# Stick-breaking value blocks first, token tile by token tile, with the norm's weight row spread by TensorE

## Chip, cores and metric

One core of a Trainium2 chip runs the kernel. The metric is the device time of one execution in microseconds (us); the times given are medians of runs. Engines: TensorE (PE) multiplies, VectorE (DVE), ScalarE (ACT) and GpSimd (POOL) compute element by element, SyncE (SP) issues most DMAs.

## Reference

A decoder block on 256 tokens of width 1024, and a second block behind it. Only the head of the first one matters here:

```
def rmsnorm(x, g):
    xf = x.astype(jnp.float32)
    y = xf * lax.rsqrt(jnp.mean(xf * xf, axis=-1, keepdims=True) + EPS)
    return (y * g.astype(jnp.float32)).astype(x.dtype)
...
        h = rmsnorm(x, norm_mix[l])
        (fq, fk, fv, ff, gq, gk, gv, gb, ga, gz, sq, sk, sv, gates) = split_projection(h @ w_in[l])
        ...
        ya = fox_attention(fq, fk, heads(fv, FOX_HEADS), logf)
        ...
        o = gated_delta_rule(l2norm(heads(cq, GDN_HEADS)), l2norm(heads(ck, GDN_HEADS)),
                             heads(cv, GDN_HEADS), g_log, beta)
        ...
        yc = stick_breaking_attention(heads(sq, SB_HEADS), heads(sk, SB_HEADS), heads(sv, SB_HEADS))
```

In the stick-breaking branch the scores z are q times k; log_keep is minus the softplus of z; its sums over the later keys are added to z, and the exp of that multiplies the values sv. In the delta rule a triangular 64 x 64 system per chunk is solved. Everything is float32.

## Kernel before

The weights stream through the core once, in 187 blocks of 1 MB, in the order of the table PHASES (name, number of blocks). Block n goes through three buffers: a DMA on SyncE's queue puts each half (512 KB) into RAW (two slots), ScalarE rounds it to HI (four slots), VectorE makes LO = RAW - HI. A product is then three matmuls: HI with x's high part XH, LO with XH, HI with XL. A slot of RAW is free for block n + 2 once LO of block n is there. HI and LO of block n + 4 are made by the calls `split_ahead` on ScalarE and VectorE, placed by hand behind the work on block n. Each engine runs its program strictly in the order in which it is written, and semaphores join them.

Blocks come in forms: f (`f_gemm`: 48 matmuls of 256 tokens, output by channel, used for gdn, sbqk and the gates) and t (`t_part` for one token tile, `t_half` for both: 24 matmuls of 512 columns, output by token, used for sbv, foxqk, foxv). Products of blocks go to the four PSUM banks ACCP; `_accumulations` says which. Small things go to the four banks SMP, in turn, in the order of the list SMALL: a name waits until the name four places before it has been taken out of its bank.

The opening: SyncE loads x in two tiles of 128 tokens, then the norm's weight row norm_mix spread over all partitions (PRE_GAIN, 512 KB written), then gdn's first two blocks, then small rows. ScalarE sums the squares, POOL forms the root, VectorE scales (`norm_scale`, two halves a tile), TensorE transposes (`norm_turn`), ScalarE copies to XH and VectorE subtracts to XL (`norm_split`, per quarter). Ahead of that TensorE runs seven warm-up products (WARM_UP).

The middle, on TensorE: six gdn blocks, four sbqk blocks with the delta rule's transposes between them, sbv block 0, the small products kk and kq (four names of SMP), sbv block 1, the scores z0 to z3, foxqk 0 to 2, `rest_sums` for two heads (waits for keep_ready), foxqk 3, the other two heads, foxv 0 and 1, the products so (exp of the sticks times SV), gate_c 0, T16, gate_c 1, the transposes fT of the fox heads.

Beside it VectorE takes kk into delta_L (DL) and kq into delta_AT (MAT), forms SP_ from z (keep_abs, then keep_ready after ScalarE's exp and ln), and solves the 16 x 16 diagonal blocks (diag_L, diag_T, 30 small instructions), whose data SyncE moves through DRAM: eight writes of delta_L, a read into diag_L, and after the solve a write and eight reads into delta_P. The weight loads behind them in SyncE's queue wait for it.

Of the kernel before, what the change touches and what calls it, by code (L numbers as in the profile page):

```python
# [52 lines left out]
    ("gdn", 6), ("sbqk", 4), ("sbv", 2), ("foxqk", 4), ("foxv", 2),  # L53
# [34 lines left out]
def _accumulations():  # L88
# [9 lines left out]
    for phase, count in PHASES:  # L98
# [84 lines left out]
def build(nc, A, out):  # L183
# [24 lines left out]
    with ctx:  # L208
# [73 lines left out]
        TINY = at("TINY", 26, [P, SEQ])  # L282
        TW = at("TW", 80, [P, KT, 12])
# [82 lines left out]
        sumsq, scaled, norm_hi = sems("sumsq scaled norm_hi")  # L366
        tiny_hi, tiny_lo, tiny_abs, tiny_ln, tiny_sp, tiny_exp = sems("tiny_hi tiny_lo tiny_abs tiny_ln tiny_sp tiny_exp")
# [156 lines left out]
        def _(sp):  # L524
# [54 lines left out]
            for j in range(RAWS, 6):  # L579
                load("gdn", Turn(j), f_block(w["w_in"], C_GQKV + 256 * j))  # L580
            load_f("sbqk", w["w_in"], C_SQ)
            load_t("sbv", w["w_in"], C_SV)
# [62 lines left out]
        def _(pool):  # L645
# [18 lines left out]

            pool.memset(BROW, 0.0).then_inc(bias_zeroed, 1)
# [130 lines left out]
        def _(pe):  # L796
# [26 lines left out]
            def t_part(phase, j, m, xh, xl, ready=None):  # L823

                chunk, half = Turn(j // 2), j % 2
                s = lo_is_ready(pe, phase, Turn(j))
                if half == 0:
                    acc_banks_free(pe, phase, chunk, m)
                for k in range(4):
                    kk = 4 * half + k  # L830
                    if ready:
                        ready(kk)
# [135 lines left out]

            for _ in range(WARM_UP):
                pe.matmul(SMP[:, 3, 0:P], IDENT[:, :], IDENT[:, :], start=True, stop=True)  # L970
            for t in range(NT):
                norm_turn("norm_mix", XS, t)

            for j in range(6):
                f_gemm("gdn", Turn(j), XH, XL, norm_ready("norm_mix", 0, 1) if j == 0 else None)
# [43 lines left out]
            t_half("sbv", 0, XH, XL)  # L1019
# [6 lines left out]
            t_half("sbv", 1, XH, XL)  # L1026

# [7 lines left out]
            for j in range(3):  # L1035
                t_half("foxqk", j, XH, XL)
# [32 lines left out]
            f_gemm("gate_c", Turn(0), XH, XL)  # L1069
# [318 lines left out]
        def _(act):  # L1388
# [71 lines left out]
            for t in range(NT):  # L1460
                act.wait_ge(x_loaded[t], 16)
                norm_square("norm_mix", t, X, XS)
            for t in range(NT):
                norm_split("norm_mix", t, XH)
                split(0, (t,))
            for n in range(1, RING):
                split(n)
            act.wait_ge(tiny_w_loaded, 16 * 2)
            copy(THI[:, :, :], TW[:, :, :], tiny_hi)


# [99 lines left out]
            split_ahead("gate_c", Turn(0))  # L1571
            take_small("T16_0", ME[:, 0], by_head(small("T16_0")))
# [337 lines left out]
        def _(dve):  # L1910
# [42 lines left out]
            def norm_scale(r, t, src, dst):  # L1953

                dve.wait_ge(pre_gain_loaded, 16 * (NORMS.index(r) + 1))
                root = root_is_ready(f"{r}.{t}")
                for half in (slice(0, DM // 2), slice(DM // 2, DM)):
                    dve.scalar_tensor_tensor(out=dst[:, t, half], in0=src[:, t, half], scalar=root,
                                             in1=PRE_GAIN[:, half], op0=ALU.mult, op1=ALU.mult).then_inc(scaled, 1)

            def norm_split(r, t, hi, lo):

                for b in range(2):
# [26 lines left out]
            for t in range(NT):  # L1990
                dve.wait_ge(x_loaded[t], 16)
                norm_scale("norm_mix", t, X, XS)
            for t in range(NT):
                norm_split("norm_mix", t, XH, XL)
                split(0, (t,))
            split(1)

# [9 lines left out]
            for n in range(2, RING):  # L2007
                split(n)
            dve.wait_ge(tiny_hi, 1)
            dve.tensor_tensor(TLO[:, :, :], TW[:, :, :], THI[:, :, :].bitcast(f32), ALU.subtract).then_inc(tiny_lo, 1)  # L2010

# [57 lines left out]
            split_ahead("sbv", Turn(0))  # L2069
# [10 lines left out]
            split_ahead("sbv", Turn(1))  # L2080
# [3 lines left out]

            dve.wait_ge(diag_loaded, 16)
# [11 lines left out]
            split_ahead("foxqk", Turn(0))  # L2097
# [4 lines left out]
            split_ahead("foxqk", Turn(1))  # L2102

            split_ahead("foxqk", Turn(2))

# [454 lines left out]
```

## Time and profile before

| what | us |
|---|---|
| median of 3 timed runs | 1183.82 (1183.72 to 1186.32) |
| the profiled execution | 1186.28 |
| its span, first to last instruction | 1184.3 |
| TensorE busy | 1158.5 (98%) |
| VectorE busy | 738.5 (62%) |
| ScalarE busy | 595.0 (50%) |

All times in rows are of the profiled execution, from the start of its span. Busy time of TensorE counts overlapping pipelined matmuls, so 98% does not mean that it is at its peak.

### The profile page before, as it was taken

To read this page: it belongs to the slowest core of one execution; us is meant where nothing else is said; L and a number is where in the kernel's file an instruction comes from. 1 tells how busy PE (TensorE), PEld (TensorE's weight loads), DVE (VectorE), ACT (ScalarE), POOL (GpSimd) and SP (SyncE) were. 2 spreads that over 40 slices of the span, in tenths; PEclk is the share of its full clock that TensorE was granted. 3 is DMA by queue.
4 is the path that set the end of the run, shared out by engine and by line. 5 is a ranking of instruction groups with operands and counts; after the bars stand their busy time and mean duration, and the time that the engine had idled before them with its cause. 6 is when DMAs were issued, how large, how long until landed. Compare 5 with 4: busy or idle time off the path is not lost.

```text
span 1184.3 us, 19550 instructions
## 1 busy us (share of the span) xinstructions
PE 1158.5 (98%) x7788; PEld 1070.6 (90%) x7788; DVE 738.5 (62%) x912; ACT 595.0 (50%) x799; POOL 96.1 (8%) x156
## 2 busy tenths in 40 slices
PE   7999999999999999999999999999999999999997
PEld 7998799999888999988999998799888899999885
DVE  5767656557766788764665544565775566554455
ACT  5675544345555665652544443464473365443352
POOL 5310211001010000000000000200400010000011
PEclk9999999999999999999999999999999999999999
DMA  8744453446553675565565646565475458655641
GB/s 238 214 128 128 145 178 107 137 148 198 197 191 114 222 218 177 177 213 178 167 209 178 194 161 211 156 217 165 123 245 179 160 149 273 191 178 178 199 139 70
DMA packets 150287, 208.77 MB, mean 176 GB/s; under 512 B 10944, under 2 KB 113485, under 8 KB 150221
## 3 DMA queue, kind: packets, MB, share of 16 engines
q1 hardware_dynamic: 147053, 199.18, 53.9%
q10 hardware_dynamic: 3072, 8.65, 2.1%
q8 instruction: 48, 0.79, 0.3%
q0 software_dynamic: 96, 0.01, 0.1%
q14 instruction: 18, 0.15, 0.0%
HBM read 206.63 MB, written 1.18 MB: 175 GB/s over the span
## 4 chain that ended last, share of the span: by engine, by line
PE 88%; DVE 6%; ACT 3%; DMA 2%; issue 1%; POOL 1%; SPq 0%; POOLq 0%; DVEq 0%; ACTq 0%
PE ACCP L799 25%; PE ACCP L801 25%; PE ACCP L800 25%; DVE LO L1922 3%; PE SMP L950 2%; PE SMP L943 2%; PE SMP L799 2%; PE SMP L800 2%; PE SMP L801 2%; ACT HI L1411 1%; DMA PRE_GAIN<-in_norm_mix_dram 1%; DMA diag_L<-scratch_diag_l 1%; DMA RAW<-in_w_out_b_dram 0%; PE ACCP L920 0%; DVE U L2444 0%
## 5 line engine op out<-in xcount | busy, mean ns | idle before, releaser
L1922 DVE TENSOR_TENSOR LO<-RAW,HI 128x1024 fp32r<-128x1024 f32 x367 | 438.3, 1233 | 238.6 <-ACT HI L1411 236.9
L1411 ACT ACTIVATE HI<-RAW 128x1024 fp32r<-128x1024 f32 x366 | 369.1, 1054 | 233.2 <-PE ACCP L801 201.5
L799 PE MATMUL ACCP<-XH,HI 128*128 128x256 f32 x1408 | 401.2, 285 | 1.9 <-DVE XL L1967 1.9
L801 PE MATMUL ACCP<-XH,LO 128*128 128x256 f32 x1408 | 399.1, 283 | 0.0
L800 PE MATMUL ACCP<-XL,HI 128*128 128x256 f32 x1408 | 399.0, 283 | 0.0
L799 PEld LDWEIGHTS ACCP<-XH,HI 128*128 128x128 f32 x1408 | 270.8, 192 | 2.4 <-DVE LO L1922 2.2
L800 PEld LDWEIGHTS ACCP<-XL,HI 128*128 128x128 f32 x1408 | 270.9, 192 | 0.0
L801 PEld LDWEIGHTS ACCP<-XH,LO 128*128 128x128 f32 x1408 | 270.8, 192 | 0.0
L799 PE MATMUL ACCP<-HI,HH 128*128 128x512 f32 x328 | 128.8, 393 | 1.9 <-DVE HL L2463 1.9
L801 PE MATMUL ACCP<-HI,HL 128*128 128x512 f32 x328 | 128.4, 392 | 0.0
L800 PE MATMUL ACCP<-LO,HH 128*128 128x512 f32 x328 | 128.3, 391 | 0.0
L799 PE MATMUL ACCP<-HI,XH 128*128 128x512 f32 x272 | 107.0, 393 | 2.3 <-ACT SV L1419 1.6
L801 PE MATMUL ACCP<-HI,XL 128*128 128x512 f32 x272 | 105.9, 390 | 0.0
L800 PE MATMUL ACCP<-LO,XH 128*128 128x512 f32 x272 | 105.9, 389 | 0.0
L676 POOL TENSOR_SCALAR STAT<-STAT 128x1 f32<-128x1 f32 (+3 forms) x30 | 10.0, 334 | 807.7 <-ACT XS L1665 461.8
L799 PEld LDWEIGHTS ACCP<-HI,HH 128*128 128x128 f32 x328 | 62.0, 189 | 14.8 <-issue 2.0
L801 PEld LDWEIGHTS ACCP<-HI,HL 128*128 128x128 f32 x328 | 61.9, 189 | 13.0
L800 PEld LDWEIGHTS ACCP<-LO,HH 128*128 128x128 f32 x328 | 62.0, 189 | 12.7
L799 PEld LDWEIGHTS ACCP<-HI,XH 128*128 128x128 f32 x272 | 51.1, 188 | 13.2 <-issue 1.7
L801 PEld LDWEIGHTS ACCP<-HI,XL 128*128 128x128 f32 x272 | 51.0, 188 | 10.8
L800 PEld LDWEIGHTS ACCP<-LO,XH 128*128 128x128 f32 x272 | 51.1, 188 | 10.1
L799 PE MATMUL SMP<-HI,XH 128*128 128x256 f32 x160 | 45.6, 285 | 1.5 <-DVE XL L1967 1.1
(375 smaller groups left out, 1320.4 us busy)
## 6 DMA issues: line engine op xcount, KB each, us to landing
RAW<-in_w_in_dram SPq DMA_DIRECT2D x104, 512.0 KB, 4.6
RAW<-in_w_up_dram SPq DMA_DIRECT2D x44, 512.0 KB, 4.5
RAW<-in_ffn_w_gate_dram SPq DMA_DIRECT2D x44, 512.0 KB, 4.5
RAW<-in_ffn_w_up_dram SPq DMA_DIRECT2D x44, 512.0 KB, 4.6
RAW<-in_ffn_w_down_dram SPq DMA_DIRECT2D x44, 512.0 KB, 4.2
RAW<-in_w_down_dram SPq DMA_DIRECT2D x22, 512.0 KB, 4.2
RAW<-in_w_out_dram SPq DMA_DIRECT2D x8, 512.0 KB, 4.2
RAW<-in_w_mkv_dram SPq DMA_DIRECT2D x8, 512.0 KB, 4.2
```

Of the source, the lines that this page charges most:

```text
L676: link(pool.tensor_scalar(mean_square, mean_square, EPS, None, ALU.add))
L799: pe.matmul(dst, lhs[0], rhs[0], start=start, stop=False)
L800: pe.matmul(dst, lhs[0], rhs[1], start=False, stop=False)
L801: return pe.matmul(dst, lhs[1], rhs[0], start=False, stop=stop)
L943: last = pe.matmul(small(name)[:, h * P:(h + 1) * P], lhs, rhs, start=True, stop=True)
L950: last = pe.transpose(small(name)[:, h * P:(h + 1) * P], source(h), IDENT[:, :])
L1411: act.activation(HI[:, n % RING, half_of(half)], RAW[:, n % RAWS, half, :], ACT.Copy).then_inc(hi_ready, 1)
L1922: dve.tensor_tensor(LO[:, s, c], RAW[:, n % RAWS, half, :], HI[:, s, c].bitcast(f32), ALU.subtract).then_inc(lo_ready[s], 1)
```

## The change

The two sbv blocks become the first of all blocks and are multiplied tile by tile: as soon as x's first tile is normed, both sbv blocks are run on it, then both on the second tile. gdn follows, on both tiles; its PSUM banks are shifted by two. SyncE's load order is x tile 0, sbv 0, x tile 1, sbv 1, the small rows, gdn. The weight row is no longer loaded spread: ScalarE's queue loads it as one row of 4 KB (GAIN_ROW), and TensorE multiplies a row of ones with it, once per 512 columns, into the idle banks 2 and 3 of ACCP, from which `norm_scale` reads it. In the middle, foxqk 0 takes the place of sbv 0, nothing stands between kq and z, and foxqk, foxv and gate_c 0 move one place ahead.

```diff
 PHASES = [
-    ("gdn", 6), ("sbqk", 4), ("sbv", 2), ("foxqk", 4), ("foxv", 2),
+    ("sbv", 2), ("gdn", 6), ("sbqk", 4), ("foxqk", 4), ("foxv", 2),
...
-                acc(phase, j, j, (j + (phase in PAIRS) * 2) % 4)
+                acc(phase, j, j, (j + (phase in PAIRS or phase == "gdn") * 2) % 4)
```

SyncE's loads:

```diff
             for t in range(NT):
                 sp.dma_start(X[:, t, :], A["x"][0, tok(t), :]).then_inc(x_loaded[t], 16)
-            sp.dma_start(PRE_GAIN[:, :], A["norm_mix"].broadcast_to([P, DM])).then_inc(pre_gain_loaded, 16)
-            for j in range(RAWS):
-                load("gdn", Turn(j), f_block(w["w_in"], C_GQKV + 256 * j))
+                load("sbv", Turn(t), t_block(w["w_in"], C_SV, t))
```

GpSimd:

```diff
+            pool.memset(ONE_ROW[:, :], 1.0).then_inc(one_row_ready, 1)
```

TensorE:

```diff
+            for b in range(2):
+                pe.matmul(ACCP[:, 2 + b, :], ONE_ROW[:, :], GAIN_ROW[:, b * 512:(b + 1) * 512], start=True, stop=True).then_inc(gain_spread, 1)
             for _ in range(WARM_UP):
                 pe.matmul(SMP[:, 3, 0:P], IDENT[:, :], IDENT[:, :], start=True, stop=True)
-            for t in range(NT):
-                norm_turn("norm_mix", XS, t)
+            for m in range(NT):
+                norm_turn("norm_mix", XS, m)
+                for j in range(2):
+                    last = t_part("sbv", j, m, XH, XL, norm_ready("norm_mix", m), by_half=m == 0)
+                    if m == 1:
+                        last.then_inc(block_done, 1)
...
-            t_half("sbv", 0, XH, XL)
+            t_half("foxqk", 0, XH, XL)
...
-            t_half("sbv", 1, XH, XL)
-
...
-            for j in range(3):
+            for j in range(1, 4):
                 t_half("foxqk", j, XH, XL)
...
-            t_half("foxqk", 3, XH, XL)
+            t_half("foxv", 0, XH, XL)
             for h in range(2, 4):
                 rest_sums(h)
-            for j in range(2):
-                t_half("foxv", j, XH, XL)
+            t_half("foxv", 1, XH, XL)
+            f_gemm("gate_c", Turn(0), XH, XL)
...
-            f_gemm("gate_c", Turn(0), XH, XL)
```

ScalarE:

```diff
+            act.dma_start(GAIN_ROW[:, :], A["norm_mix"]).then_inc(gain_row_loaded, 16)
+            act.wait_ge(x_loaded[0], 16)
+            norm_square("norm_mix", 0, X, XS)
+            split(0)
+            norm_split("norm_mix", 0, XH)
+            act.wait_ge(x_loaded[1], 16)
+            norm_square("norm_mix", 1, X, XS)
+            split(1)
+            norm_split("norm_mix", 1, XH)
...
-            split_ahead("sbv", Turn(0))
-
-            for half in range(2):
-                split_ahead("sbv", Turn(1), (half,))
-                for h in ((0,), (1, 2, 3))[half]:
-                    take_small(f"z{h}", Z[:, h, :], small(f"z{h}")[:, 0:384])
-            take_t("sbv", 0, SV)
             split_ahead("foxqk", Turn(0))
+            for h in range(HEADS):
+                take_small(f"z{h}", Z[:, h, :], small(f"z{h}")[:, 0:384])
...
+            take_t("foxv", 0, FV)
+            split_ahead("foxv", Turn(1))
             for h in range(HEADS):
                 small_is_taken(act, f"rc{h}")
             act.activation(Z[:, :, :], Z[:, :, :], ACT.Exp).then_inc(stick_ready, 1)
-            take_t("foxv", 0, FV)
-            split_ahead("foxv", Turn(1))
```

VectorE:

```diff
+            dve.wait_ge(x_loaded[0], 16)
+            norm_scale("norm_mix", 0, X, XS)
+            for half in range(2):
+                split(0, (half,))
+                norm_split("norm_mix", 0, XH, XL, (half,))
             split(1)
+            dve.wait_ge(x_loaded[1], 16)
+            norm_scale("norm_mix", 1, X, XS)
+            norm_split("norm_mix", 1, XH, XL)
...
-            split_ahead("sbv", Turn(0))
+            split_ahead("foxqk", Turn(0))
...
-            split_ahead("sbv", Turn(1))
             for h in range(HEADS):
                 small_is_taken(dve, f"z{h}")
             dve.scalar_tensor_tensor(out=SP_[:, :, :], in0=Z[:, :, :], scalar=-1.0, in1=Z[:, :, :], op0=ALU.mult, op1=ALU.max).then_inc(keep_abs, 1)
 
+            split_ahead("foxqk", Turn(1))
             dve.wait_ge(diag_loaded, 16)
...
             ins.then_inc(diag_solved, 1)
-            split_ahead("foxqk", Turn(0))
             dve.wait_ge(keep_ln, 1)
```

TensorE at the opening, before: four quarters of transposes, then gdn's first block (small_taken are the banks of SMP that XL's subtractions free, lo_ready0 is LO of block 0, scaled is VectorE's scaling).

```order
L950 MATMUL SMP<-IDENT,XS 128x128 [waits scaled]
L950 MATMUL SMP<-IDENT,XS 128x128 x3
L950 MATMUL SMP<-IDENT,XS 128x128 [waits scaled]
L950 MATMUL SMP<-IDENT,XS 128x128 x3
L799 MATMUL ACCP<-XH,HI 128x256 [waits small_taken2,small_taken0,lo_ready0]
L800 MATMUL ACCP<-XL,HI 128x256
L801 MATMUL ACCP<-XH,LO 128x256
```

The same place in the changed kernel, from its first matmul.

```order
L973 MATMUL ACCP<-GAIN_ROW,ONE_ROW 128x512 [waits gain_row_loaded,one_row_ready,masks_ready]
L973 MATMUL ACCP<-GAIN_ROW,ONE_ROW 128x512
L975 MATMUL SMP<-IDENT 128x128 x7
L951 MATMUL SMP<-IDENT,XS 128x128 [waits scaled]
L951 MATMUL SMP<-IDENT,XS 128x128 x3
L951 MATMUL SMP<-IDENT,XS 128x128 [waits scaled]
L951 MATMUL SMP<-IDENT,XS 128x128 x3
L798 MATMUL ACCP<-HI,XH 128x512 [waits small_taken0,lo_ready0]
L799 MATMUL ACCP<-LO,XH 128x512
L800 MATMUL ACCP<-HI,XL 128x512
```

The gain products stand ahead of the warm-ups, and the first weight product follows two quarters of transposes and waits for one quarter of x (small_taken0) instead of two.

TensorE around the scores z, before: the end of sbv block 1, z0 to z3 (L1032 and L1033), the start of foxqk 0.

```order
L801 MATMUL ACCP<-HI,XL 128x512
L1032 MATMUL SMP<-SQK 128x256 [waits acc_taken3,acc_taken2,small_taken2,acc_taken1,acc_taken0]
L1033 MATMUL SMP<-SQK 128x128
L1032 MATMUL SMP<-SQK 128x256 [waits small_taken3]
L1033 MATMUL SMP<-SQK 128x128
L1032 MATMUL SMP<-SQK 128x256 [waits small_taken0]
L1033 MATMUL SMP<-SQK 128x128
L1032 MATMUL SMP<-SQK 128x256 [waits small_taken1]
L1033 MATMUL SMP<-SQK 128x128
L799 MATMUL ACCP<-HI,XH 128x512 [waits acc_taken0,lo_ready0]
```

The same place in the changed kernel: the end of kq (L944), z (L1039 and L1040), the start of foxqk 1.

```order
L944 MATMUL SMP<-QKF 128x128 [waits small_taken1,small_taken3]
L944 MATMUL SMP<-QKF 128x128 x3
L1039 MATMUL SMP<-SQK 128x256 [waits acc_taken3,acc_taken2,small_taken2,acc_taken1,acc_taken0]
L1040 MATMUL SMP<-SQK 128x128
L1039 MATMUL SMP<-SQK 128x256 [waits small_taken3]
L1040 MATMUL SMP<-SQK 128x128
L1039 MATMUL SMP<-SQK 128x256 [waits small_taken0]
L1040 MATMUL SMP<-SQK 128x128
L1039 MATMUL SMP<-SQK 128x256 [waits small_taken1]
L1040 MATMUL SMP<-SQK 128x128
L798 MATMUL ACCP<-HI,XH 128x512 [waits lo_ready1]
```

What moved is the block between kq and z: none stands there now. The banks small_taken2, 3, 0 and 1 are those of kk0, kk1, kq0 and kq1.

VectorE behind kq, before: the kq products, LO of a block, the absolute value of z, the diagonal solve.

```order
L2079 TENSOR_TENSOR delta_AT<-SMP,delta_B 128x512 [waits small_done] x2
L1922 TENSOR_TENSOR LO<-RAW,HI 128x1024 [waits hi_ready] x2
L2083 SCALAR_TENSOR_TENSOR SP__72<-Z 128x1536 [waits small_taken0,small_taken1,small_taken3,small_taken2]
L2092 TENSOR_TENSOR diag_term<-diag_L,diag_T 64x15 [waits diag_zeroed,diag_loaded]
L2093 TENSOR_TENSOR diag_T<-diag_T,diag_term 64x15 [waits dve_step]
```

The same place in the changed kernel.

```order
L2097 TENSOR_TENSOR delta_AT<-SMP,delta_B 128x512 [waits small_done] x2
L2100 SCALAR_TENSOR_TENSOR SP__72<-Z 128x1536 [waits small_taken0,small_taken1,small_taken3,small_taken2]
L1932 TENSOR_TENSOR LO<-RAW,HI 128x1024 [waits hi_ready] x2
L2110 TENSOR_TENSOR diag_term<-diag_L,diag_T 64x15 [waits diag_zeroed,diag_loaded]
L2111 TENSOR_TENSOR diag_T<-diag_T,diag_term 64x15 [waits dve_step]
```

LO (now of the block four behind foxqk 1) stands behind the absolute value and ahead of the solve; the LO that stood between the solve and the keep sums is gone from there.

## Rows read from the trace of the kernel before

**Rows 1.** The page, part 1: busy time, share of the span, instructions.
```profile
PE 1158.5 (98%) x7788; PEld 1070.6 (90%) x7788; DVE 738.5 (62%) x912; ACT 595.0 (50%) x799; POOL 96.1 (8%) x156
```

**Rows 2.** TensorE's waits, whole span: us in total, times, longest.
```profile
PE SMP L1045 <- DVE SP__72 L2101: 2.2, 1, 2.2
```

**Rows 3.** Timeline, TensorE, opening: start, us, line, operation, count, idle before.
```profile
4.03 3.36 PE L970 MATMUL SMP<-IDENT 128*128 128x128 f32 x14 [4.03 <-POOL IDENT L655]
9.09 3.64 PE L950 MATMUL SMP<-IDENT,XS 128*128 128x128 f32 x16 [1.70 <-DVE XS L1958]
14.64 0.35 PE L799 MATMUL ACCP<-XH,HI 128*128 128x256 f32 x1 [1.91 <-DVE XL L1967]
```

**Rows 4.** Timeline of ScalarE, GpSimd and VectorE, opening.
```profile
4.45 1.06 ACT L1427 ACTIVATE XS<-X 128x1024 f32<-128x1024 f32 x1 [2.36 <-DMA X<-in_x_dram]
6.10 0.57 POOL L677 TENSOR_TENSOR STAT<-STAT 128x1 f32<-128x1 f32 x1
8.28 2.84 DVE L1958 SCALAR_TENSOR_TENSOR XS<-X,STAT,PRE_GAIN 128x512 f32<-128x512 f32 x4 [8.28 <-DMA PRE_GAIN<-in_norm_mix_dram]
11.04 1.38 DVE L1967 TENSOR_TENSOR XL<-SMP,XH 128x512 fp32r<-128x512 f32 x2
```

**Rows 5.** Windows of TensorE: length, busy (instructions), granted clock, DMA share, GB/s.
```profile
14.60:15.80 1.20, 1.16 (x10) 1.00 1.07 45
16.40:19.20 2.80, 2.80 (x14) 0.50 0.97 279
122.00:124.00 2.00, 2.00 (x7) 0.50 0.56 108
```

**Rows 6.** DMA issues from 95 to 125: count, KB each, median us to landing.
```profile
scratch_diag_l<-delta_L SPq DMA_DIRECT2D x8, 8.0 KB, 1.7
```

**Rows 7.** Timeline, TensorE, middle: kk and kq, z, first foxqk block, rest_sums.
```profile
89.86 3.73 PE L943 MATMUL SMP<-QKF 128*128 128x128 f32 x32
98.88 0.59 PE L1032 MATMUL SMP<-SQK 128*128 128x256 f32 x2
103.23 0.47 PE L799 MATMUL ACCP<-HI,XH 128*128 128x512 f32 x1 [1.57 <-ACT SV L1419]
121.97 0.69 PE L1045 MATMUL SMP<-BIG_NOT_BEFORE_R,IDENT_R 128*128 128x384 f32 x1 [2.17 <-DVE SP__72 L2101]
```

**Rows 8.** Timeline, ScalarE, middle.
```profile
90.05 2.18 ACT L1411 ACTIVATE HI<-RAW 128x1024 fp32r<-128x1024 f32 x2 [0.92 <-PE ACCP L801]
110.87 1.47 ACT L1547 ACTIVATE SP__72<-SP__72 128x1536 f32<-128x1536 f32 x1
115.05 1.06 ACT L1419 ACTIVATE X<-ACCP 128x512 f32<-128x512 f32 x2
116.00 2.01 ACT L1411 ACTIVATE HI<-RAW 128x1024 fp32r<-128x1024 f32 x2
```

**Rows 9.** Timeline, VectorE, middle.
```profile
94.44 2.15 DVE L2074 SCALAR_TENSOR_TENSOR delta_L<-SMP,STAT,delta_A 128x128 f32<-128x128 f32 x8
96.51 1.28 DVE L2079 TENSOR_TENSOR delta_AT<-SMP,delta_B 128x512 f32<-128x512 f32 x2
102.74 1.76 DVE L2083 SCALAR_TENSOR_TENSOR SP__72<-Z 128x1536 f32<-128x1536 f32 x1
109.18 0.17 DVE L2092 TENSOR_TENSOR diag_term<-diag_L,diag_T 64x15 f32<-64x15 f32 x1 [4.68 <-DMA diag_L<-scratch_diag_l]
116.45 2.35 DVE L1922 TENSOR_TENSOR LO<-RAW,HI 128x1024 fp32r<-128x1024 f32 x2
```

**Rows 10.** SyncE's queue in the timeline, then the chain of waits.
```profile
96.68 3.66 SPq L595 DMA_DIRECT2D scratch_diag_l<-delta_L  x8
103.18 5.98 DMA diag_L<-scratch_diag_l
```

**Rows 11.** Timeline, VectorE and ScalarE, behind foxv.
```profile
142.88 4.54 DVE L1982 TENSOR_TENSOR X<-X,STAT 128x1024 f32<-128x1024 f32 x2 [3.87 <-POOL STAT L677]
144.40 1.08 ACT L1419 ACTIVATE FV<-ACCP 128x512 f32<-128x512 f32 x2 [0.63 <-PE ACCP L801]
```

More of the change, by code:

```diff
@@ L282, in build @@
         TINY = at("TINY", 26, [P, SEQ])
+        GAIN_ROW, ONE_ROW = at("GAIN_ROW", 64, [1, DM]), at("ONE_ROW", 68, [1, P])
         TW = at("TW", 80, [P, KT, 12])
@@ L578, in _ @@
             sp.dma_start(TW[:, :, 4:12], tiny_rows[:, :, C_GB:C_GB + 8]).then_inc(tiny_w_loaded, 16)
-            for j in range(RAWS, 6):
-                load("gdn", Turn(j), f_block(w["w_in"], C_GQKV + 256 * j))
+            load_f("gdn", w["w_in"], C_GQKV)
             load_f("sbqk", w["w_in"], C_SQ)
-            load_t("sbv", w["w_in"], C_SV)
             load_t("foxqk", w["w_in"], C_FQ)
@@ L821, in f_gemm, with t_part @@
                 f_part(phase, t, xh, xl, slice(0, SEQ), ready).then_inc(block_done, 1)
-            def t_part(phase, j, m, xh, xl, ready=None):
+            def t_part(phase, j, m, xh, xl, ready=None, by_half=False):
                 chunk, half = Turn(j // 2), j % 2
-                s = lo_is_ready(pe, phase, Turn(j))
+                s = lo_is_ready(pe, phase, Turn(j), half=0 if by_half else 1)
                 if half == 0:
@@ L830, in t_part @@
                     kk = 4 * half + k
+                    if by_half and k == 2:
+                        lo_is_ready(pe, phase, Turn(j))
                     if ready:
@@ L1458, in softmax_exp @@
                 ins.then_inc(bank_of(name), 1)
[L1460 to L1466, printed above, removed]
+            act.dma_start(GAIN_ROW[:, :], A["norm_mix"]).then_inc(gain_row_loaded, 16)
[7 more added lines that the diff above has]
+            norm_split("norm_mix", 1, XH)
+            for n in range(2, RING):
                 split(n)
@@ L1469, in _ @@
             copy(THI[:, :, :], TW[:, :, :], tiny_hi)
+            split_ahead("sbv", Turn(0))
+            acc_is_done(act, "sbv", Turn(0))
+            for m in range(NT):
+                copy(SV[:, m], acc("sbv", Turn(0), m), acc_bank("sbv", Turn(0), m))
+            split_ahead("sbv", Turn(1))
             def conv_silu(j):
@@ L1562, in _ @@
             act.activation(Z[:, :, :], Z[:, :, :], ACT.Exp).then_inc(stick_ready, 1)
-            take_t("foxv", 0, FV)
-            split_ahead("foxv", Turn(1))
+            act.wait_ge(heads_ready, 4)
+            gates("gate_c", 0, G, 2)
+            split_ahead("gate_c", Turn(0))
             for g in range(2):
@@ L1953, in norm_scale, with norm_split @@
             def norm_scale(r, t, src, dst):
-                dve.wait_ge(pre_gain_loaded, 16 * (NORMS.index(r) + 1))
                 root = root_is_ready(f"{r}.{t}")
-                for half in (slice(0, DM // 2), slice(DM // 2, DM)):
+                for b, half in enumerate((slice(0, DM // 2), slice(DM // 2, DM))):
+                    if r == "norm_mix":
+                        dve.wait_ge(gain_spread, b + 1)
+                        gain = ACCP[:, 2 + b, :]
+                    else:
+                        dve.wait_ge(pre_gain_loaded, 16 * NORMS.index(r))
+                        gain = PRE_GAIN[:, half]
                     dve.scalar_tensor_tensor(out=dst[:, t, half], in0=src[:, t, half], scalar=root,
-                                             in1=PRE_GAIN[:, half], op0=ALU.mult, op1=ALU.mult).then_inc(scaled, 1)
-            def norm_split(r, t, hi, lo):
-                for b in range(2):
+                                             in1=gain, op0=ALU.mult, op1=ALU.mult).then_inc(scaled, 1)
+            def norm_split(r, t, hi, lo, quarters=range(2)):
+                for b in quarters:
                     name = f"{r}.{t}{b}"
@@ L2005, in _ @@
             link(dve.tensor_scalar(col("mq_norm"), col("mq_norm"), DH ** -0.5, None, ALU.mult))
[L2007 to L2010, printed above, removed]
+            split_ahead("sbv", Turn(1))
             for j in range(6):
@@ L2112, in _ @@
                 stick_arg(h)
-            split_ahead("foxqk", Turn(3))
+            split_ahead("foxv", Turn(0))
             for h in range(2, 4):
```

24 lines of the change are left out of this document (11 added, 13 removed).

## Prediction

> **What bounds the kernel now.** I read the page's engine shares first: TensorE is busy 98% of the span [rows 1], so a change pays only where TensorE stands or runs slowly, and costs wherever it makes TensorE stand. The view of TensorE's waits names the larger one in the middle: 2.2 us for the keep sums [rows 2], and the timeline 1.57 us for a PSUM bank that ScalarE had not yet emptied [rows 7]. It shows the rest too, at the opening: the warm-up products end at about 7.4, the transposes start at 9.09, and the first weight product only at 14.64 [rows 3]. The reader should see there that VectorE began scaling at 8.28, although the root of tile 0 was ready at 6.67: it had waited for the spread weight row [rows 4]. The windows give TensorE's clock: granted 1.00 (2.4 GHz) at 14.6, then 0.50 (1.2 GHz) from 16.4 to 19.2 after an opening with gaps, and 0.50 again at 122 to 124, after the 2.17 us wait [rows 5, 7]. In the slow stretch 14 products started in 2.8 us, against 10 in 1.2 us before it; the whole of it (about 15.9 to 19.2) cost some 1.6 us, and the one at 122 some 1.5.
>
> After 14.64 TensorE is nearly unbroken, so I count how late it is, phase by phase, against that timeline.
>
> **Term 1, the opening.** Removed: the 512 KB spread of the weight row. Added: a 4 KB load on ScalarE's queue, one POOL memset (0.1 us) and two K=1 products of 512 columns. No row shows such a load; the nearest are the 8 KB writes that landed in 1.7 us [rows 6] and the weight row itself, wanted by VectorE at 8.28 [rows 4]. So the row lands between about 3 and 8; I take 4, since it is small and early, and TensorE starts at 4.1 as now. A warm-up product is two passes of 128 columns; 14 passes took 3.36 us, 0.24 each [rows 3]. Four passes of 512 columns are then at most 3.8 us: the two halves of the gain are there at 6.0 and 7.9. The seven warm-ups behind them take 3.4 us if the clock stays low, half that if it rises; I take 10.0 for their end. VectorE scales half by half from 6.7 (0.75 each), the second half at 7.9. Transposes of the first quarter end at 10.9, ScalarE copies (0.6), VectorE subtracts (0.69, half of the row of 1.38) [rows 4]: 12.2, and the first block's first half starts, 2.4 us earlier than now.
>
> It doesn't run through. ScalarE turns to x's second tile only then (1.06 and 0.19, then two splits of 1.0 each), so the second block's low half is ready at 15.8; TensorE, done with the first at 15.0, waits 0.8, finishes at 18.5, transposes tile 1 (16 passes, 1.8), waits 0.5 for the subtraction, and ends both blocks of tile 1 at 26.3 (5.5 us of products). The two blocks are 11.0 us of work (three such blocks took 16.6, below), so this equals an unbroken start at 15.3. Now it is 14.64 plus 1.6 of slow clock, 16.2. Gain 0.9, plus 0.3 because the same two blocks now cost 5.7 each in the middle: **-1.2**. Bounds: -4.1 (start at 12.2 with no wait and no slow stretch behind), +2 (row lands near 8).
>
> **Term 2, the bank wait goes.** The first foxqk block waited 1.57 us for ScalarE's copies of SV [rows 7]; SV is now taken long before. **-1.6**.
>
> **Term 3, a new wait for z.** Let F be the moment when TensorE begins the kk products: 89.9 now, behind the first sbv block; in the change behind foxqk's first. kk and kq take 3.4. Now sbv's second block (5.7) stands behind them; in the change z follows at once. Each z takes the bank of one kk or kq, and VectorE empties those late: ScalarE's split begins at F+0.15 and takes 2.18, VectorE's low half follows, and its delta_L rows run at F+4.5 to F+6.6, its products on kq until F+7.9 [rows 8, 9]. So z0 starts at F+5.6, z1 at F+6.6, z3 at F+7.8. The four z end at F+8.5, where 3.4 + 2.6 (98.9 to 101.7 [rows 7]) would give F+6.0. **+2.5**. VectorE's program ahead of kk is unchanged in kind, so I see no cover for this one.
>
> **Term 4, the keep wait grows.** From the end of z, F+8.5: ScalarE copies the last z (0.5), VectorE forms the absolute value 1.76 [rows 9]: F+10.8. ScalarE's exp to the first foxqk copy is 4.2 (110.87 to 115.05), the copies 0.95, its split 2.0 [rows 8]: F+18.0. The order now puts that block's low half ahead of the diagonal solve: F+19.3. The diagonal data should be there: VectorE's delta_L ends at F+6.6, the eight writes issue in 3.7, the read took 6.0 behind a weight load [rows 10], so about F+18. The solve takes 7.3 (109.18 to 116.45), the keep sums 3.2 (118.8 to 121.97) [rows 7, 9]: F+29.8. TensorE has only three foxqk blocks to do, 103.23 to 119.80, that is 16.6 [rows 7]: it is free at F+25.1 and waits 4.8 us, not 2.2. **+2.6**. Bounds 0 (solve starts at F+16.7) and +4. Late next are the loads of gate_c's first two blocks, which SyncE issues behind the solve. By the same count they are split at about F+36 and F+41, wanted at F+48 and F+56: covered.
>
> **Term 5, gate_c block 0 behind foxv.** It takes a PSUM bank that foxv's first chunk just filled. ScalarE's two copies took 1.08 and began at once [rows 11]; the bank is free 0.6 later: **+0.6**. In return the exp of the sticks is hidden under gate_c; it was hidden before too.
>
> **Term 6, the transposes of HT.** VectorE waits 3.87 for POOL's root and scales for 4.54, ending at 147.4 [rows 11], 3 us behind the end of foxv. In the change it starts these some 7 to 10 us later relative to foxv, since its splits wait for late weights; ScalarE's gates, its next split and its copies of the stick outputs stand behind, and the banks the transposes want come free at about the moment they want them: 0 to 1.5, I take **+0.7**.
>
> **Term 7, the clock.** The keep wait is twice as long, and z's wait (2.2 us in one piece) resembles the one that was followed by the low level, while the 1.57 us wait was not. Slow products behind z are hidden by the keep wait; behind keep they are not: 0 to 2.5, I take **+0.9**.
>
> Phases from out_c on are the same program. Sum: -1.2 - 1.6 + 2.5 + 2.6 + 0.6 + 0.7 + 0.9 = **+4.5 us**. The profiled execution took 1186.28 with a span of 1184.3; the three timed runs have their median at 1183.82, so the sum goes on the median: 1188.3. A measurement of this kernel can tell about 0.3% (3.6 us) from no change.
>
> **Rivals.** *The opening runs clean.* The trace shows that TensorE could have had x 1.6 us earlier, and with the clock up from 12.2 term 1 is -4.1, term 7 nothing: +0.7, or 1184.5, not slower. Against it stand the waits of 0.8 and 0.5 worked out above. *The new waits don't come.* If VectorE empties kk and kq before z wants them and keep stays at 2.2, terms 3, 4 and 7 vanish: -1.5, or 1182.3; with a clean opening 1179.4, faster. The deciding point is F+3.4: VectorE would have to finish with kk0 by then, and in the rows it starts at F+4.5. *The low clock stays through the opening.* Transposes and warm-ups then take twice as long and the first 24 products too: q0's subtraction comes 2.2 later, and tile 0's products cost up to 2.7 more, part of it in waits: +3, or 1191.3. In the rows 16 transpose passes took 3.64 us (0.23 each), the low pace, yet the products at 14.6 ran at the high level [rows 3, 5]: the clock rose while nothing but warm-ups and transposes had run. The Trainium skill ("TensorE: Matmul & The Clock Gate", Part 4: PE-mode transpose) says that transposes don't count as activity for raising the clock. By that rule the clock would still be low at the first products, as in this rival; the trace of before doesn't agree, since the level was 1.00 at 14.6, but the change puts two real products ahead, so neither reading makes it much likelier.
>
> **Chances.** Forecast 0.55 (its own range 1185 to 1192), clean opening 0.18, no new waits 0.15, low clock 0.12. Above 1187.4 lie the low clock and most of the forecast (0.45): 0.57. Below 1180.3 lies half of the case without waits and a sliver of the clean opening: 0.11. The rest is 0.32. The range of 8 in 10 runs from 1180.5 to 1193: it takes in most of the case without waits, and at the top the low clock with the upper bound of term 4.
>
> **What would show it.** Right: first ACCP product of XH near 12.2; gdn's first block near 26.3; a wait of about 2.2 before the z products on VectorE's delta_L; a wait near 4.8 before the keep sums; 0.6 before gate_c's first block. Wrong: no wait at z (then VectorE's program is ahead of where I place it), or a solve that starts before the foxqk split. The forecast fails most easily if the opening gains more than 3 us.

## The result

The changed kernel takes 1193.01 us (median of 4 runs, 1190.49 to 1194.48); the kernel before takes 1183.77 in the same measurement (4 runs, 1182.28 to 1186.32). The ratio is 1.0083, 95% interval 1.0067 to 1.0098: 9.2 us slower, where the forecast was 4.5. The profiled execution took 1190.49, with a span of 1188.8; it is the fastest of the four, and the profiled one of before (1186.28) is one of the slowest of its kernel. So the two traces differ by only 4.5 us. A second trace of each differs by 8.9, the size of the measured loss; most of the reading below uses those two. They are called *before, second trace* (label b_again) and *after, second trace* (a_again).

**Busy time** is what it was [rows 1]. The page of the changed kernel:

```profile
PE 1159.6 (98%) x7792; PEld 1069.4 (90%) x7792; DVE 739.0 (62%) x912; ACT 595.4 (50%) x799; POOL 97.7 (8%) x157
```

TensorE is busy 1.1 us longer in a span that is 4.5 us longer; busy time counts slow products too, so the clock is in it, and the rest is standing. **TensorE's waits** behind its start, in the first 200 us (us in total, times, longest), answer to [rows 2]:

```profile
PE SMP L1052 <- DVE SP__72 L2118: 5.1, 1, 5.1
PE SMP L1039 <- DVE delta_L L2092: 2.1, 1, 2.1
PE ACCP L798 <- DVE XL L1982: 1.7, 2, 1.1
PE ACCP L798 <- ACT FV L1425: 0.8, 1, 0.8
```

L1052 is rest_sums waiting for the keep sums, L1039 z waiting for the kk bank, and the last row gate_c's first block. All three are where the prediction put them, with 4.8, 2.2 and 0.6. The wait for SV of [rows 7] is not in the list. **The opening**, TensorE's timeline, beside [rows 3]:

```profile
4.06 3.77 PE L973 MATMUL ACCP<-GAIN_ROW,ONE_ROW 1*128 1x512 f32 x4 [4.06 <-POOL IDENT L653]
7.76 3.35 PE L975 MATMUL SMP<-IDENT 128*128 128x128 f32 x14
10.91 1.91 PE L951 MATMUL SMP<-IDENT,XS 128*128 128x128 f32 x8
13.48 0.47 PE L798 MATMUL ACCP<-HI,XH 128*128 128x512 f32 x1 [0.65 <-DVE XL L1982]
```

The row had landed before TensorE wanted it. The seven warm-ups ran at the low pace to the end, so the transposes begin at 10.91 and not at 10.0. The first weight product is at 13.48, not 12.2, and the products behind it run at full pace, 0.23 from start to start (kk_first below has another opening). **The middle**, beside [rows 7]:

```profile
100.82 3.73 PE L944 MATMUL SMP<-QKF 128*128 128x128 f32 x32
106.66 0.67 PE L1039 MATMUL SMP<-SQK 128*128 128x256 f32 x2 [2.11 <-DVE delta_L L2092]
109.59 0.48 PE L798 MATMUL ACCP<-HI,XH 128*128 128x512 f32 x1
131.28 0.69 PE L1052 MATMUL SMP<-BIG_NOT_BEFORE_R,IDENT_R 128*128 128x384 f32 x1 [5.10 <-DVE SP__72 L2118]
```

With F = 100.82 the z products begin at F+5.8 (predicted F+5.6) and rest_sums at F+30.5 (predicted F+29.8). VectorE shows the order behind both waits, beside [rows 9]: the split of the weights, then delta_L; later another split, then the first step of the solve.

```profile
103.12 2.36 DVE L1932 TENSOR_TENSOR LO<-RAW,HI 128x1024 fp32r<-128x1024 f32 x2
105.40 2.15 DVE L2092 SCALAR_TENSOR_TENSOR delta_L<-SMP,STAT,delta_A 128x128 f32<-128x128 f32 x8
118.53 2.36 DVE L1932 TENSOR_TENSOR LO<-RAW,HI 128x1024 fp32r<-128x1024 f32 x2 [6.27 <-ACT HI L1417]
120.81 0.16 DVE L2110 TENSOR_TENSOR diag_term<-diag_L,diag_T 64x15 f32<-64x15 f32 x1
```

**The clock** is where the traces of one kernel part ways. Windows (length, busy and instructions, granted clock, DMA share, GB/s) of the first trace of before,

```profile
16.00:18.50 2.50, 2.50 (x13) 0.50 0.95 258
122.00:125.00 3.00, 3.00 (x10) 0.50 0.53 91
886.50:889.50 3.00, 3.00 (x8) 0.50 0.46 171
```

of its second trace,

```profile
16.00:18.50 2.50, 2.50 (x14) 0.50 0.92 259
122.00:124.00 2.00, 1.67 (x10) 1.00 0.80 197
886.00:889.00 3.00, 3.00 (x15) 1.00 0.39 127
```

of the first trace of the changed kernel,

```profile
106.50:109.50 3.00, 2.79 (x15) 1.00 0.05 8
131.50:133.50 2.00, 2.00 (x8) 0.50 1.11 353
```

and of its second trace.

```profile
16.00:18.50 2.50, 2.40 (x11) 1.00 1.05 342
108.00:111.00 3.00, 3.00 (x12) 0.50 0.13 14
132.00:136.00 4.00, 3.37 (x11) 0.50 0.89 256
```

In both traces of before the level falls to 0.50 (1.2 GHz) in the opening. The stretches at 122 and 886, some 1.5 us each, stood in the first one only. The changed kernel has none in the opening in either trace, one of 7 us behind the keep wait in both, and in the second trace one on the z products too. The second trace of before has the same two waits in the middle (keep 2.56, SV 1.57) without a low level behind them.

### The profile page after: what moved, and what is told of

It is laid out like the page before. It is cut to its first block, busy times and chain, and to the rows that moved or that the text cites. A ratio compares the mean times of both kernels' runs of the same rounds, so it can differ in the third digit from the quotient of the medians.

```text
span 1188.8 us, 19557 instructions
## 1 busy us (share of the span) xinstructions
PE 1159.6 (98%) x7792; PEld 1069.4 (90%) x7792; DVE 739.0 (62%) x912; ACT 595.4 (50%) x799; POOL 97.7 (8%) x157
## 4 chain that ended last, share of the span: by engine, by line
PE 85%; DVE 7%; ACT 4%; issue 1%; POOL 1%; DMA 1%; POOLq 0%; DVEq 0%; ACTq 0%
PE ACCP L798 25%; PE ACCP L800 24%; PE ACCP L799 24%; DVE LO L1932 3%; PE SMP L951 2%; ACT HI L1417 2%; PE SMP L798 2%; PE SMP L800 2%; PE SMP L799 2%; PE SMP L944 1%; POOL STAT L676 1%; DMA RAW<-in_w_in_dram 1%; DMA RAW<-in_w_out_b_dram 0%; PE ACCP L921 0%; DVE XS L1973 0%
## 5 line engine op out<-in xcount | busy, mean ns | idle before, releaser
L798 PEld LDWEIGHTS ACCP<-HI,HH 128*128 128x128 f32 x328 | 61.6, 188 | 14.6 <-issue 2.2
```

The costliest lines, as they stand in the source:

```text
L798: pe.matmul(dst, lhs[0], rhs[0], start=start, stop=False)
```

## Experiments

Each is compared with the kernel before on its own chip; ratios are to before, so that kernels timed on different chips can be set side by side.

**The two kernels again.** No edit.

> The changed kernel, unaltered, timed again on one chip beside the kernel before, for its spread and a second trace. Known: +4.2 us between the two profiled executions (1190.49 against 1186.28), +9.2 between the medians. Theory A (clock): the waits before z (2.1) and before the keep sums (5.1) are the same in each execution, but the clock falls after them, or in the opening, in some executions and not in others; then this trace shows the same waits within 0.3 us and more slow clock than the first one, and the median is +8 to +10. Rival B (noise between the two sets of runs): the median comes to +4 to +6. Rival C (the opening): its first gdn block starts 2 us or more later than at 27.2.

> The kernel before, unaltered, for a second trace. Its first profiled execution (1186.28) was 2.5 above its median. Theory A: the second trace has the same two waits (1.6 and 2.2) and less slow clock, in the opening or behind the keep wait (each stretch cost about 1.5). Rival B: same clock stretches, and a span within 1 us of 1184.3. The ratio of its times to those of the kernel before must be 1.000 within 0.1%.

The changed kernel: 1191.68, ratio 1.0075 (1.0058 to 1.0092). Before against itself: 1182.21, ratio 0.9999 (0.9988 to 1.0011). Over the whole execution the mean granted clock was 0.994 or 0.995 in all six of the changed kernel, and 0.992 to 0.998, with its median at 0.996, in the 17 of before beside them: 0.2% of 1184 is 2.4 us. The loss repeats, as theory A had it, and part of it is in the clock. The mean clock also says how usual the first trace of before is: it had 0.994, and 14 of those 17 had 0.996 or more.

**keep_first**: the keep sums ahead of the split and the solve on VectorE.

```
             keep_abs ...
+            dve.wait_ge(keep_ln, 1)
+            ... the three keep sums ... .then_inc(keep_ready, 1)
             split_ahead("foxqk", Turn(1))
             dve.wait_ge(diag_loaded, 16)
             ... the solve ...
-            ... the keep sums ...
```

> The changed kernel with VectorE's three keep-sum instructions moved ahead of the foxqk split and the diagonal solve. The keep sums can then start when ScalarE's ln is ready (about F+15) and end by F+18.5, before TensorE is free at F+25. Theory A: the wait of 5.1 and the slow clock behind it (2.4) go, -7 to -8 us against the changed kernel, so +1 to +2.5 against the kernel before. Rival D (the wait only moves: the solve and its weight loads, now 3 us later, stall gate_c): -3 to -5 only, with a new wait of 2 us or more behind foxv.

1191.89, ratio 1.0081 (1.0062 to 1.0100): nothing gained. Rival D, that the wait only moves, was right in kind, but expected 3 to 5 us to be left. TensorE's waits behind 90 us:

```profile
PE ACCP L798 <- ACT FV L1425: 5.5, 1, 5.5
PE SMP L951 <- DVE YL L2003: 1.2, 1, 1.2
```

The keep wait is gone, z waits 2.1 as in the changed kernel, and gate_c's first block waits 5.5 instead of 0.8. SyncE's queue and ScalarE say why:

```profile
113.08 0.53 SPq L595 DMA_DIRECT2D diag_L<-scratch_diag_l  x1
129.34 0.46 SPq L597 DMA_DIRECT2D scratch_diag_t<-diag_T  x1
129.84 1.17 SPq L535 DMA_DIRECT2D RAW<-in_w_in_dram  x2
134.77 1.06 ACT L1417 ACTIVATE HI<-RAW 128x1024 fp32r<-128x1024 f32 x1 [15.33 <-DMA RAW<-in_w_in_dram]
146.09 1.06 ACT L1425 ACTIVATE FV<-ACCP 128x512 f32<-128x512 f32 x2
```

SyncE stands from 113.6 to 129.3 for the solve, and the weights of gate_c's block 0 are queued behind it. ScalarE waits 15.3 us for them, and its copy of FV, which frees the bank, stands behind that split. The real chain is: solve, SyncE's loads, ScalarE's order, PSUM bank. It was there in the changed kernel too, hidden behind the keep wait: ScalarE stood 4.4 us for TensorE ahead of the same copy (149.06). Here TensorE is done with foxv 7.7 us earlier (141.3 against 149.0), while ScalarE is free for the copy only at 146.1, where it was free at 144.6 there.

**kk_first**: the kk and kq work of VectorE ahead of its split of block 16, four behind foxqk 0 (`split_ahead("foxqk", Turn(0))` moved behind the kq loop).

> The changed kernel with VectorE's kk and kq work moved ahead of the split of the block four behind foxqk 0. VectorE then empties kk's banks by F+4.2 instead of F+6.6. The wait before z (2.1) should go. The chain from the end of z to the keep sums is 21.3 us long and shifts with it, and TensorE's work between them does too, so the keep wait stays at about 5. Theory A: -2.3 us, and less than that by nothing hidden. Rival E (the keep wait is bound by the diagonal data, not by z): the keep wait grows by the 2.3 that z gives, and the time stays.

1188.36, ratio 1.0045 (1.0028 to 1.0061), 3.3 us below the changed kernel on the same chip. z follows kq at once (105.56), with the clock up; the keep wait is 5.52. The two waits together are 1.6 shorter (5.5 against 2.1 and 5.0), so some 1.7 us came back otherwise; I put it on the clock on z, as the difference, not as a reading.

This trace holds something else. Its edit touches nothing in the opening, but the first products are slow there:

```profile
13.48 0.77 PE L798 MATMUL ACCP<-HI,XH 128*128 128x512 f32 x1 [0.65 <-DVE XL L1982]
14.04 0.63 PE L799 MATMUL ACCP<-LO,XH 128*128 128x512 f32 x1
14.47 0.63 PE L800 MATMUL ACCP<-HI,XL 128*128 128x512 f32 x1
```

The step is 0.43 until 17.0, and gdn and everything behind it come 1.2 us later than in the first trace of the changed kernel (kk at 101.98 against 100.82). The seven other traces with this opening ran at full pace from 13.48 or so, with gdn's first block at 27.0 to 27.3. So the changed kernel too has a low pace in its opening in some executions.

**warm**: the changed kernel with products that nobody reads, in its two pauses.

```
+            for _ in range(9): pe.matmul(ACCP[:, 2, 0:P], IDENT, IDENT)     (ahead of z)
             for h in range(HEADS):
...
+            acc_is_taken(pe, "foxqk", Turn(0))
+            for _ in range(21): pe.matmul(ACCP[:, 0, 0:P], IDENT, IDENT)    (ahead of the keep wait)
             pe.wait_ge(keep_ready, 1)
```

> The changed kernel with products that nobody reads put into its two new pauses: 9 of 128 columns ahead of the z products and 21 ahead of the keep sums, so that TensorE has something to do while it waits. No wait is shortened. If the low clock behind the waits is a cost of its own (stretches of 3.4 us at half pace, in two traces of three on the z products and behind the keep sums in all three, each worth 1.5 to 3.4 us of products), it vanishes and the time falls by 2 to 4 us against the changed kernel on the same chip, to about 1188.5, with no stretch at 0.50 between 100 and 145 us. If only the length of the waits counts, the time stays within 0.7 us of it.

1188.14, ratio 1.0042 (1.0029 to 1.0055), against 1.0075 without the fillers: 3.9 us by the ratios (1.4 to 6.4 by their intervals together). Between the profiled spans it is 4.3 against the second trace (1186.3 and 1190.6) and 2.5 against the first (1188.8), which had no low level on z. TensorE's timeline and windows:

```profile
104.29 2.17 PE L1038 MATMUL ACCP<-IDENT 128*128 128x128 f32 x18
125.92 4.85 PE L1049 MATMUL ACCP<-IDENT 128*128 128x128 f32 x42
131.22 0.45 PE L1057 MATMUL SMP<-BIG_NOT_BEFORE_R,IDENT_R 128*128 128x384 f32 x1 [0.44 <-DVE SP__72 L2123]
```

```profile
108.00:111.00 3.00, 3.00 (x19) 1.00 0.16 17
131.50:135.00 3.50, 3.50 (x21) 1.00 0.79 224
```

z starts at 106.49 and rest_sums at 131.22, no earlier than in the first trace without fillers (106.66 and 131.28). The waiting is all there, but filled, and the level doesn't fall behind it. So about 4 us is the price of the low clock behind the two waits, beside the waits themselves.

**keep_early**: keep_first, and SyncE issues gate_c's loads 0 and 1 before it waits for the solve. **both_early**: that with kk_first. **both_early2**: that with gate_c's load 2 ahead of the eight reads of the solved diagonal.

```
             sp.dma_start(DIAG_L ...).then_inc(diag_loaded, 16)
+            for j in range(2): load("gate_c", Turn(j), ...)                 (and no longer behind the solve)
             sp.wait_ge(diag_solved, 1)
             sp.dma_start(diag_t ..., DIAG_T ...).then_inc(diag_stored, 16)
+            load("gate_c", Turn(2), ...)                                    (both_early2 alone)
```

> The changed kernel with the keep sums ahead of the block split and the solve (as in keep_first), and with SyncE issuing the loads of gate_c's blocks 0 and 1 before it waits for the solve instead of behind it. If the late loads behind the solve are what ate the gain of keep_first, the wait of gate_c's first block (5.5 us there) falls to 1 us or less, the keep wait stays away, and the time falls by 5 to 7 us against the changed kernel: 1185 to 1187. If the gain goes on to a next wait (the T16 transposes behind a later solve, or the transposes of HT), it falls by at most 2 us and that wait shows 3 us or more.

> As keep_early, and with the kk and kq work of VectorE ahead of the low half of block 16 (as in kk_first), so that z has no wait either. If both waits, with their low clock, are the whole loss of the change and the removed SV-bank wait a real gain, this ends 8 to 11 us below the changed kernel: 1181 to 1183.5, not slower than the kernel before and up to 1 us faster. If the opening of the change costs something too, it stays 2 us or more above the kernel before.

> As both_early, and with gate_c's third load ahead of the eight reads of the solved diagonal on SyncE's queue. There a wait of 2.1 us for ScalarE's copy of FV was left, behind a split that waited 9.2 us for that load, with a stretch at 0.50 after it. If that is the last of the chain, the wait falls to 0.8 or less and the time by 2 to 3.6 us against both_early, to 1181.6 to 1183.2, level with the kernel before or up to 1 us faster. If the eight reads, now later, hold up the T16 transposes, the time stays at 1185.

keep_early: 1188.33, ratio 1.0044 (1.0032 to 1.0056). both_early: 1185.21, ratio 1.0016 (1.0004 to 1.0029). both_early2: 1179.82, ratio 0.9975 (0.9963 to 0.9986). keep_early gained less than I expected, 3.7 us, for gate_c still waited 2.1 and z kept its wait. both_early came to 7.0 us below the changed kernel by the ratios, where I expected 8 to 11. both_early2 went further down than expected, 1179.82 against 1181.6 to 1183.2. In both_early ScalarE shows the next load in the chain, two places ahead of its copy of FV; both_early2 stands behind it:

```profile
137.75 1.06 ACT L1420 ACTIVATE HI<-RAW 128x1024 fp32r<-128x1024 f32 x1 [9.19 <-DMA RAW<-in_w_in_dram]
```

```profile
132.60 1.06 ACT L1421 ACTIVATE HI<-RAW 128x1024 fp32r<-128x1024 f32 x1 [3.96 <-DMA RAW<-in_w_in_dram]
138.87 1.09 ACT L1429 ACTIVATE FV<-ACCP 128x512 f32<-128x512 f32 x2 [3.37 <-PE ACCP L804]
```

In the second it is ScalarE that waits for TensorE at FV, and gate_c's wait is back at the 0.8 that the shared bank costs. In its window from 140 to 144 the granted clock is 1.00, where both_early had 0.50 from 142. The step gave 4.9 us by the ratios' difference for a wait 1.3 us shorter. By the two traces the clock gave more back than the wait did: both_early's had a low stretch behind the wait and another at 886, and this one's had neither. The T16 transposes come at 148.06, 3.3 us before the 151.39 of before's second trace. both_early2 is 0.25% below the kernel before. It doesn't say what the value blocks at the head are worth by themselves, since the kernel before was not given orders and loads fitted in the same way.

**gain_only**: the kernel before, its weight row spread by TensorE (4 KB on ScalarE's queue and the two K=1 products, in place of the 512 KB load).

> The kernel before with one part of the change alone: the first norm's weight row comes as 4 KB and is spread by two TensorE products into idle PSUM banks, in place of the 512 KB load. By my term for the opening the scaling starts 1.6 us earlier and the second half waits for the second product (7.9): the first weight product comes 1 to 1.5 us earlier than 14.6 and the time falls by about 1 us (ratio 0.999). If the weights' own arrival sets the start, the first product stays within 0.4 us of 14.6 and the time is the same.

1183.67, ratio 1.0006 (0.9996 to 1.0016): no change that can be told, and the expected gain of 1 us is not there. TensorE's timeline:

```profile
10.90 3.20 PE L952 MATMUL SMP<-IDENT,XS 128*128 128x128 f32 x16
16.41 0.36 PE L801 MATMUL ACCP<-XH,HI 128*128 128x256 f32 x1 [2.30 <-DVE XL L1979]
```

Against [rows 3] the transposes are 1.8 later and so is the first product, since the two spread products (3.8 us) push the warm-ups back. VectorE scales at 7.04 instead of 8.28, which is worth nothing, for TensorE isn't free until 10.9. A kernel with the spread products in place of the warm-ups was not run.

**row_not_spread**: the changed kernel with the 512 KB load again, first on ScalarE's queue.

> The changed kernel without its spread by TensorE: the weight row comes as the 512 KB load again, but first on ScalarE's queue instead of behind x on SyncE's; the value blocks stay first. In gain_only the two spread products pushed the warm-ups and transposes back, and the phases behind came 1.7 us later. If that is so here too, the transposes come before 10.9 and the first weight product at 12.5 or less instead of 13.48, and the time falls by 1 to 1.5 us against the changed kernel. If the weights' halves and ScalarE's order set the opening of the change, its first gdn block starts within 0.4 us of 27.1 as now and the time is the same.

1191.55, ratio 1.0063 (1.0050 to 1.0076), not told apart from the changed kernel's 1.0075. TensorE's timeline and a window:

```profile
9.36 1.97 PE L950 MATMUL SMP<-IDENT,XS 128*128 128x128 f32 x8 [1.98 <-DVE XS L1963]
12.41 0.76 PE L797 MATMUL ACCP<-HI,XH 128*128 128x512 f32 x1 [1.08 <-DVE XL L1972]
12.97 0.63 PE L798 MATMUL ACCP<-LO,XH 128*128 128x512 f32 x1
13.40 0.63 PE L799 MATMUL ACCP<-HI,XL 128*128 128x512 f32 x1
```

```profile
12.50:15.50 3.00, 3.00 (x7) 1.00 1.17 163
```

The first product comes 1.1 us earlier, as expected, but a product of 512 columns takes 0.43 until 15.5 (the pace of 1.2 GHz), and gdn's first block starts at 27.33, where the changed kernel has 27.1 to 27.3. That is my rival of a low clock through the opening. The pause of 2 us ahead of the transposes isn't needed for it: in kk_first's trace TensorE had worked unbroken from 4.06 to the end of the transposes, and the low pace was there as well, to 17.0. With one trace of this kernel, the run doesn't tell whether the low pace belongs to its opening or to that execution.

**before_keep**: the kernel before with its own keep sums ahead of the solve. **before_keep_fill**: that, with 8 products that nobody reads between the transposes of the opening and the first weight product.

> The kernel before with one edit of its own: the keep sums ahead of the diagonal solve on VectorE, as in keep_first. If the keep wait of 2.2 to 2.6 us was a plain loss, it goes, with the low clock that stood behind it in some executions: 2.5 to 3.5 us below the kernel before, 1179 to 1180 (ratio 0.9975). If the later solve hands the wait on, as it did in the changed kernel (5.5 us at gate_c's first block), the time is the same within 1 us and a wait for a block of foxv or gate_c shows 2 us.

> As before_keep, and with 8 products of 128 columns that nobody reads between the transposes of the opening and the first weight product, where TensorE stands 2.2 us and the stretch at 0.50 of 15.5 to 18.9 follows. If that stretch is the price of the pause, it goes and the time falls by a further 1.6 us against before_keep: about 1177.5 to 1178.5. If the low level comes from something else in the opening, the stretch stays and the time is that of before_keep.

1189.38 (1.0046, 1.0033 to 1.0059) and 1189.47 (1.0051, 1.0038 to 1.0064): both slower by some 6 us (5.4 and 6.0 by the ratios), where I expected 3 us faster, or, had the wait only moved, no change. The keep wait is gone and a larger one stands at the stick products, with the level at 0.50 for 6.8 us behind it:

```profile
PE SMP L1066 <- ACT Z L1562: 7.0, 1, 7.0
```

```profile
124.26 0.46 SPq L599 DMA_DIRECT2D scratch_diag_t<-diag_T  x1
129.39 1.06 ACT L1411 ACTIVATE HI<-RAW 128x1024 fp32r<-128x1024 f32 x1 [12.74 <-DMA RAW<-in_w_in_dram]
144.44 1.48 ACT L1562 ACTIVATE Z<-Z 128x1536 f32<-128x1536 f32 x1
```

The store behind the solve is at 124.26 (116.56 in the first trace of before), the loads behind it are late by as much, and ScalarE reaches the exp of Z at 144.4 (142.28 in that trace). The old order, solve first, was the cheaper place for the wait. The fillers decided nothing: the opening of before_keep had no low level in its trace either (1.00 from 16 to 18.5), and its phases behind came 1.3 us earlier than in before's second trace. The stretch in the opening is in some traces of the old opening and not in others, so its cause stays open.

## Why the prediction was wrong

The direction was right, the mechanisms were mostly right, and the size was half. The two second traces allow the sum to be taken apart. The blocks that the one has done and the other has not count 5.53 each (three took 16.6 [rows 7]). The changed kernel's lead or lag over before is then -0.2 us at the first transposes of the convolution (71.07 and 60.22, two blocks apart), +2.1 at the first foxqk block behind z (110.81 and 103.16, one block apart), +4.8 at rest_sums (132.63 and 122.33, one block), and +8.7 at T16 (160.07 and 151.39, the same blocks). Behind T16 both take 1030 us.

**Term 1, the opening: -1.2 forecast, -0.2 measured.** The step that failed here is the end of the warm-ups: I took 10.0, between the low pace and a clock that rises, and it was 11.1. The spread products themselves cost what I said (3.8). In gain_only's trace spreading the row costs before's opening 1.8 us, though its time doesn't show it (1.0006). Without the spread, row_not_spread's first product is 1.1 earlier and its opening ends no sooner. A low stretch or a low pace in the opening shifts all that follows by 1.2 or 1.3 us from one execution to another (kk_first, before_keep), as much as this term is off.

**Term 2, -1.6: right.** The SV wait stands with 1.57 in both traces of before and in none of the changed kernel.

**Term 3, +2.5: right**, 2.1 measured. kk_first confirms the place: VectorE's split ahead of delta_L.

**Term 4, +2.6: right as a size** (4.98 against 2.56 in the second traces, so 2.4). But I named late next the loads of gate_c "covered". For the changed kernel as it is that holds, since gate_c waits 0.8 for its bank alone. For the keep sums moved up it does not, as keep_first showed: 4.4 us of slack were left at the copy of FV, and TensorE came 7.7 us earlier.

**Term 5, +0.6: right**, 0.8. **Term 6, +0.7: wrong**, the fT transposes didn't wait.

**Term 7, the clock, +0.9 forecast, some 4 measured: the step that failed.** In the second traces the stretch on z is 3.4 us long and that behind keep covers 6.0 us of products (132.6 to 138.7): at half pace 1.7 and 3.0, so 4.7 us, and the middle of before has none to set against it. warm measured 3.9 by leaving every wait in place and keeping the level up. Three things went wrong in the term. I wrote that slow products behind z are hidden by the keep wait. They aren't, for the chain to the keep sums starts from the last z. The second trace, beside 109.59 and 131.28 above, has z beginning 0.2 earlier and ending 1.2 later, and rest_sums 1.35 later behind a wait of the same length:

```profile
110.81 0.71 PE L798 MATMUL ACCP<-HI,XH 128*128 128x512 f32 x1
132.63 0.69 PE L1052 MATMUL SMP<-BIG_NOT_BEFORE_R,IDENT_R 128*128 128x384 f32 x1 [4.98 <-DVE SP__72 L2118]
```

I let one low stretch of about the old size stand behind keep, as in the trace of before; but a wait twice as long drew a stretch twice as long, 129 to 136 in place of 121.7 to 125. And I booked only an increase over a trace in which before already paid 1.5 us at 122 [rows 5]; in most executions it doesn't pay that, by the mean clocks above. It was wrong to put a sum made against that one execution on the median. That the sum met the first two spans (+4.5) was in part luck: at T16 they were already 5.7 apart (158.25 against 152.57), and the stretch at 886, which no term held, took 1.2 back. With 1.5 and 1.5 for the stretches that only that trace of before had, and 1.7 for the one on z that the first trace of the changed kernel lacked, 4.5 becomes 9.2, which is an account and not a proof, since the medians are over executions that no trace shows.

Sum of the measured terms: -0.2 - 1.6 + 2.1 + 2.4 + 0.8 + 0 + 4.7 = 8.2, against 8.9 between the spans; the 0.7 left lies in pieces too small to name.

**The rivals.** The opening didn't run clean, and the new waits came. The low clock through the opening didn't come in the two traces of the changed kernel, but it did in kk_first, with the same opening, and in row_not_spread. In kk_first it cost 1.2 us and not the 3 that I gave it, for the warm-ups ran at the low pace in the other traces too (3.35 or 3.36 us for 14 passes), and so did most of the transposes. The Trainium skill's sentence that transposes don't count as activity ("TensorE: Matmul & The Clock Gate", Part 4: PE-mode transpose) would fit row_not_spread; it doesn't fit before, whose products at 14.6 were fast with only warm-ups and transposes ahead [rows 3, 5]. Nor does it part kk_first from the seven traces that did the same work ahead of the same products and ran them at full pace. No run here shows what decides it.

## What to carry to other kernels

Price a new wait of TensorE twice: its length, and the slow products behind it. Here two waits of 2.1 and 5.0 us cost 4 us of clock on top, and filling them with idle products gave it back. A slow stretch on work that a later wait hangs on isn't hidden by that wait. Before putting a sum on the median, look for low-clock stretches in the one trace that could be missing in the next execution, and take them out of the baseline. When a wait is moved in an engine's order, follow the DMA queue that stands behind it too: the keep sums gained nothing ahead of the solve (or lost 6 us) until SyncE's loads were taken from behind it.

## What the hardware showed that I had not expected

- Whether the level falls behind a pause of 2.1 to 2.6 us differs between executions of one program. It fell behind before's keep wait of 2.17 and not behind the same wait of 2.56; it fell on z behind 2.12 us in the second trace of the changed kernel and not behind 2.11 in the first (it fell in three of the five traces with that wait). Behind 5 to 7 us it fell in all seven traces.
- The stretch behind 5.1 us was 7 us long, that behind 2.1 us 3.4. In keep_first's trace a wait of 5.5 had one of 3.4, at a mean clock of 0.996 for the whole execution; three others of that kernel had 0.992.
- The granted clock in the rows can read 1.00 while products run at the pace of 1.2 GHz: 0.43 a product of 512 columns from 13.0 to 15.5 in row_not_spread and from 14.0 to 17.0 in kk_first, 0.23 behind that. In an opening the step from product to product tells more than that column.
